# Turning attention probabilities on VectorE in 32 by 32 blocks, two heads at a time, instead of on TensorE through a PSUM bank

## The reference

```
proj = rms_norm_2(x, norm_g) @ w_in             # 2048 -> 11264 columns: q k v z_a u_b v_b z_b g_a g_b
q, k = rms_norm_2 per head of 128               # 8 heads
att = moba_attention(q, k, v)                   # 256 tokens are one block of 256: plain causal attention
y_a = (att * silu(z_a)) @ w_proj_a
sgu = spatial_gating(gelu(u_b), gelu(v_b), ...)
y_b = (sgu * silu(z_b)) @ w_proj_b
x + (sigmoid(g_a) * y_a + sigmoid(g_b) * y_b) @ w_out
```

## Time and profile before

| | |
|---|---|
| median of three runs | 2683.2 us |
| span of the profiled execution, first to last instruction | 2681.3 us |
| TensorE busy | 2675.3 us (100%) |
| VectorE busy | 1907.4 us (71%) |
| ScalarE busy | 1293.7 us (48%) |
| DMA | 192 GB/s mean, 56.6% of 16 engines on the weight queue |
| granted TensorE clock over the span | 1.000 |

### The profile page before, as it was taken

One profiled execution on the slowest core, in us unless ns is written; L12 is line 12 of the kernel. 1 busy time (PEld: TensorE's weight loads), 2 busy tenths in 40 slices (PEclk: granted clock), 3 DMA queues, 4 the chain that ended last, 5 costly groups with the idle time before them and its releaser, 6 DMA issues.

```text
span 2681.3 us, 31135 instructions
## 1 busy us (share of the span) xinstructions
PE 2675.3 (100%) x11969; PEld 2215.8 (83%) x11969; DVE 1907.4 (71%) x2594; ACT 1293.7 (48%) x1635; POOL 289.4 (11%) x263
## 2 busy tenths in 40 slices
PE   9999999999999999999999999999999999999999
PEld 7888888888888888888888888888888888888887
DVE  6887867666766777776777676667668867765564
ACT  7765544444444454444544444444445546544442
POOL 4741100000000010000100000000011001000000
PEclk9999999999999999999999999999999999999999
DMA  8555665555655556555556555556555655555554
GB/s 258 186 173 185 209 203 188 189 188 190 205 187 191 202 184 208 195 197 195 182 191 205 200 189 188 189 189 204 188 188 180 210 182 175 174 201 191 188 188 157
DMA packets 268148, 515.58 MB, mean 192 GB/s; under 512 B 8498, under 2 KB 28260, under 8 KB 267492
## 3 DMA queue, kind: packets, MB, share of 16 engines
q1 hardware_dynamic: 267732, 513.34, 56.6%
q10 hardware_dynamic: 272, 0.26, 0.0%
HBM read 511.47 MB, written 2.10 MB: 192 GB/s over the span
## 4 chain that ended last, share of the span: by engine, by line
PE 99%; DMA 0%; DVE 0%; SPq 0%; DVEq 0%; issue 0%
PE bank L819 33%; PE bank L821 32%; PE bank L820 32%; PE bank L870 0%; PE bank L888 0%; PE bank L1050 0%; DMA x_res<-in_x 0%; DMA w_raw<-in_ab_w_in 0%; PE bank L1011 0%; PE bank L1064 0%; PE bank L1037 0%; PE bank L1071 0%; PE bank L1079 0%; PE bank L1080 0%; PE bank L1038 0%; PE bank L1078 0%
## 5 line engine op out<-in xcount | busy, mean ns | idle before, releaser
L798 DVE TENSOR_TENSOR w_lo<-w_raw,w_hi 128x1024 fp32r<-128x1024 f32 x950 | 1182.1, 1264 | 471.8 <-ACT w_hi L780 465.8
L780 ACT ACTIVATE w_hi<-w_raw 128x1024 fp32r<-128x1024 f32 x954 | 973.3, 1056 | 594.5 <-PE bank L821 419.6
L819 PE MATMUL bank<-w_hi,A_lo 128*128 128x512 f32 x2432 | 952.2, 392 | 0.7 <-DVE w_lo L788 0.7
L821 PE MATMUL bank<-w_hi,A_hi 128*128 128x512 f32 x2432 | 947.1, 389 | 0.0
L820 PE MATMUL bank<-w_lo,A_hi 128*128 128x512 f32 x2432 | 946.6, 389 | 0.0
L819 PE MATMUL bank<-w_hi,B_lo 128*128 128x512 f32 x1408 | 548.7, 390 | 0.0
L821 PE MATMUL bank<-w_hi,B_hi 128*128 128x512 f32 x1408 | 547.9, 389 | 0.0
L820 PE MATMUL bank<-w_lo,B_hi 128*128 128x512 f32 x1408 | 547.8, 389 | 0.0
L819 PEld LDWEIGHTS bank<-w_hi,A_lo 128*128 128x128 f32 x2432 | 456.7, 188 | 96.4 <-DVE w_lo L788 2.1
L821 PEld LDWEIGHTS bank<-w_hi,A_hi 128*128 128x128 f32 x2432 | 456.5, 188 | 95.5
L820 PEld LDWEIGHTS bank<-w_lo,A_hi 128*128 128x128 f32 x2432 | 456.8, 188 | 93.2
(11 more groups left out here) (180 smaller groups left out, 1005.5 us busy)
## 6 DMA issues: line engine op xcount, KB each, us to landing
w_raw<-in_ffn_w SPq DMA_DIRECT2D x256, 1024.0 KB, 5.1
w_raw<-in_w_in SPq DMA_DIRECT2D x88, 1024.0 KB, 5.0
w_raw<-in_sc_w_in SPq DMA_DIRECT2D x48, 1024.0 KB, 5.1
w_raw<-in_ab_w_out SPq DMA_DIRECT2D x16, 1024.0 KB, 5.0
w_raw<-in_sc_w_out SPq DMA_DIRECT2D x16, 1024.0 KB, 5.0
w_raw<-in_w_out SPq DMA_DIRECT2D x16, 1024.0 KB, 5.1
w_raw<-in_ab_w_in SPq DMA_DIRECT2D x26, 512.0 KB, 5.0
w_raw<-in_ab_w_in SPq DMA_DIRECT2D x8, 1024.0 KB, 5.1
```

What stands on the lines that cost most here:

```text
L780: e.activation(w_hi[:, s % SPLIT_SLOTS, :], raw_step(s), ACT.Copy).then_inc(hi_made, 1)
L798: e.tensor_tensor(w_lo[:, slot, :], raw_step(s), w_hi[:, slot, :].bitcast(F32), ALU.subtract).then_inc(lo_made, 1)
L819: e.matmul(ps, lo[:, kt, tok], wh, start=first, stop=False)
L821: ins = e.matmul(ps, hi[:, kt, tok], wh, start=False, stop=last)
```

## The change

The probabilities of two heads, which lie side by side in `scores_flat` as six blocks of 128 by 128, are turned by VectorE. One instruction takes 32 partitions and a column strip of 32 from each of the six blocks (32 by 192 elements) and writes them transposed to `both_probs`. A pair needs 16 instructions, spread over five steps (3, 3, 3, 3 and 4). TensorE's 24 transposes, the eight uses of an auxiliary bank for their results and ScalarE's eight copies go. `probs_made` is now said by VectorE, once for a pair, behind the last of the 16.

The placement by `ATT_RATE` (0.76 tasks a step) is replaced by a fixed plan of ten steps a pair. Pair p begins at step f = 10p: scores at f and f+1, exp at f+2 and f+3, turn at f+4 to f+8, values at f+9 and f+10. Step f+10 is also the first of the next pair. The last values stand in step 40.

Scores of a head no longer wait for TensorE's turn of head h-2, but for `probs_made` of the pair before, on VectorE itself. The first turn of a pair waits for the exp of its second head and for the last values of the pair before, because `both_probs` has one copy.

```
@@ -126,16 +126,21 @@
...
-ATT_TASKS = []
-for _h in range(HEADS + 1):
-    ATT_TASKS += [("scores", _h)] * (_h < HEADS) + [("turn", _h - 1)] * (_h > 0)
-    ATT_TASKS += [("exp", _h)] * (_h < HEADS) + [("values", _h - 1)] * (_h > 0)
-ATT_RATE = 0.76
+PAIR_STEPS = 10
+PAIR_TURNS = 5
+ATT_AT = {}
+for _pair in range(HEADS // 2):
+    _first = PAIR_STEPS * _pair
+    for _n in range(2):
+        ATT_AT.setdefault(_first + _n, []).append(("scores", 2 * _pair + _n))
+        ATT_AT.setdefault(_first + 2 + _n, []).append(("exp", 2 * _pair + _n))
+        ATT_AT.setdefault(_first + 4 + PAIR_TURNS + _n, []).append(("values", 2 * _pair + _n))
+    for _n in range(PAIR_TURNS):
+        ATT_AT.setdefault(_first + 4 + _n, []).append(("turn", (_pair, _n)))
 
 
 def att_tasks(r, i):
-    step = 8 * (r - 8) + i
-    return ATT_TASKS[int(ATT_RATE * step):int(ATT_RATE * (step + 1))] if 8 <= r < 14 else []
+    return ATT_AT.get(8 * (r - 8) + i, [])
...
...
@@ -317,7 +320,7 @@
         small = sbuf("small", 512)
         neg_half = sbuf("neg_half", 16)
         z = sbuf("z", Z_SLOTS * NT * CH).rearrange("p (s t c) -> p s t c", s=Z_SLOTS, t=NT)
-        prod_rows = sbuf("tap_product", 2 * TOK)
+        prod_rows = sbuf("tap_product", 2 * 3 * P)
         scores_flat = sbuf("scores", 2 * 3 * P)
         halves = {}
         for name in ("A", "B"):
...
@@ -338,7 +341,7 @@
         band0 = gain_row[:, 0:4 * TOK].rearrange("p (g t) -> p g t", g=4)
         band1 = gain_row[:, 4 * TOK:4 * TOK + 4 * P].rearrange("p (g t) -> p g t", g=4)
         pool_w = acc_flat[:, 0:D].rearrange("p (g c e) -> p g c e", g=4, c=2)
-        tap_slots = [prod_rows, scores_flat[:, 0:2 * TOK]]
+        tap_slots = [prod_rows[:, 0:2 * TOK], scores_flat[:, 0:2 * TOK]]
         SPAD = SHORT_K - 1
         short_in = conv_in_flat[:, 0:GK * (TOK + SPAD)].rearrange("p (b t) -> p b t", b=GK)
         short_out = conv_out_flat[:, 0:GK * TOK].rearrange("p (b t) -> p b t", b=GK)
...
@@ -355,7 +358,8 @@
         x_T = conv_out_flat[:, GK * TOK:(GK + 2) * TOK].rearrange("p (k t) -> p k t", k=2)
         ws_T = ws_flat.rearrange("p (g c) -> p g c", g=HEADS)
         scores = scores_flat.rearrange("p (s c) -> p s c", s=2)
-        probs_T = prod_rows
+        both_scores = scores_flat.rearrange("p (b t) -> p b t", b=6)
+        both_probs = prod_rows.rearrange("p (b t) -> p b t", b=6)
         merged = acc
 
         small_at, small_cols = {}, {}
...
@@ -438,7 +442,7 @@
                               [("gelu", 8), ("gelu", 9), ("gelu", 10)] + [(11, tt) for tt in tiles] +
                               [("gelu", 12)] + [(13, tt) for tt in tiles])
         exp_made = signal("exp_made", [(h,) for h in range(HEADS)])
-        probs_made = signal("probs_made", [(h,) for h in range(HEADS)])
+        probs_made = signal("probs_made", [(pair,) for pair in range(HEADS // 2)])
 
         dve_took = signal("dve_took", [(c, tt) for c in range(N_CHUNKS) if evicted_by(c) == "DVE" for tt in tiles])
         lo_cast = signal("lo_cast", CAST)
...
@@ -1064,20 +1068,14 @@
                 e.matmul(ps[:, 0:TOK], q_T[:, h, P:TOK], k_T[:, h, :], start=True, stop=True)
                 e.matmul(ps[:, TOK:3 * P], q_T[:, h, 0:P], k_T[:, h, 0:P], start=True,
                          stop=True).then_inc(aux_filled("sc", h), 1)
-            elif task == "turn":
-                b4 = aux_begin("pt", h)
-                e.wait_ge(exp_made.sem, exp_made.of(h))
-                for b in range(3):
-                    ins = e.transpose(b4[:, b * P:(b + 1) * P], scores[:, h % 2, b * P:(b + 1) * P], ident)
-                ins.then_inc(aux_filled("pt", h), 1)
             elif task == "values":
                 b4 = aux_begin("av", h)
-                e.wait_ge(probs_made.sem, probs_made.of(h))
+                e.wait_ge(probs_made.sem, probs_made.of(h // 2))
                 e.wait_ge(act_took.sem, act_took.of(C_L2 + 5, 1))
-                c = slice(h * HD, (h + 1) * HD)
-                e.matmul(b4[:, 0:HD], probs_T[:, 2 * P:3 * P], v_tok[:, 0, c], start=True, stop=True)
-                e.matmul(b4[:, HD:2 * HD], probs_T[:, 0:P], v_tok[:, 0, c], start=True, stop=False)
-                e.matmul(b4[:, HD:2 * HD], probs_T[:, P:2 * P], v_tok[:, 1, c], start=False,
+                c, b = slice(h * HD, (h + 1) * HD), 3 * (h % 2)
+                e.matmul(b4[:, 0:HD], both_probs[:, b + 2, :], v_tok[:, 0, c], start=True, stop=True)
+                e.matmul(b4[:, HD:2 * HD], both_probs[:, b, :], v_tok[:, 0, c], start=True, stop=False)
+                e.matmul(b4[:, HD:2 * HD], both_probs[:, b + 1, :], v_tok[:, 1, c], start=False,
                          stop=True).then_inc(aux_filled("av", h), 1)
 
 
...
@@ -1344,11 +1342,6 @@
                             ins = e.activation(part, part, ACT.Exp, bias=cols(2, "bias", h)[:, n:n + 1], scale=SCALE,
                                                accum_out=cols(2, "total", h)[:, n:n + 1])
                         ins.then_inc(exp_made(h), 1)
-                    elif task == "turn":
-                        e.wait_ge(aux_filled.sem, aux_filled.of("pt", h))
-                        if h > 0:
-                            e.wait_ge(aux_filled.sem, aux_filled.of("av", h - 1))
-                        e.activation(probs_T[:, 0:3 * P], aux_bank("pt", h)[:, 0:3 * P], ACT.Copy).then_inc(probs_made(h), 1)
                 if (r, i) in AO_AT:
                     j = AO_AT.index((r, i))
                     e.wait_ge(ao_turned.sem, ao_turned.of(j))
...
@@ -2062,7 +2055,22 @@
                                                  ALU.add, ALU.mult)
                 ins.then_inc(sgu_made(j, tt), 1)
 
+        def turn_probs(e, pair, n):
+
+            if n == 0:
+                e.wait_ge(exp_made.sem, exp_made.of(2 * pair + 1))
+                if pair > 0:
+                    e.wait_ge(aux_filled.sem, aux_filled.of("av", 2 * pair - 1))
+            for m in range(16 * n // PAIR_TURNS, 16 * (n + 1) // PAIR_TURNS):
+                here, there = (slice(32 * q, 32 * q + 32) for q in divmod(m, 4))
+                ins = e.transpose(both_probs[there, :, here], both_scores[here, :, there])
+            if n == PAIR_TURNS - 1:
+                ins.then_inc(probs_made(pair), 1)
+
         def dve_attention(e, task, h):
+            if task == "turn":
+                turn_probs(e, *h)
+                return
             s = scores[:, h % 2, :]
             parts = (s[:, TOK:3 * P], s[:, 0:TOK])
             if task == "scores":
...
@@ -2070,7 +2078,7 @@
                 e.wait_ge(set_up.sem, set_up.of("mask2"))
                 e.wait_ge(aux_filled.sem, aux_filled.of("sc", h))
                 if h >= 2:
-                    e.wait_ge(aux_filled.sem, aux_filled.of("pt", h - 2))
+                    e.wait_ge(probs_made.sem, probs_made.of(h // 2 - 1))
                 e.tensor_tensor(s, aux_bank("sc", h)[:, 0:3 * P], mask, ALU.add).then_inc(masked(h), 1)
                 e.wait_ge(masked.sem, masked.of(h))
                 e.reduce_max(top[:, 0:1], parts[0], axis=AXIS.X)
```

More of the change, by code:

```diff
@@ L513, in aux_done @@
                 return conv_fed.sem, conv_fed.of(*key)
-            said = {"win": pooled_made, "ln": ln_made, "silu": aff_made, "bg": y_made, "sgu": sgu_made, "sc": masked, "pt": probs_made}
+            said = {"win": pooled_made, "ln": ln_made, "silu": aff_made, "bg": y_made, "sgu": sgu_made, "sc": masked}
             if kind in said:
```

32 lines of the change are left out of this document (10 added, 22 removed).

## The result

The changed kernel takes 2697.44 us (median of 5 runs, 2695.3 to 2697.6) against 2683.2 (now 5 runs too, 2682.73 to 2683.88): ratio 1.0050, 95% interval 1.0039 to 1.0060. It is 14.2 us slower. The forecast was 2692.0 with a range of 2686 to 2698, so time and direction are inside it, but the likeliest case, 2689 to 2695, gave only 8.8 us and was missed. The missing five are a rival's. The profiled execution has a span of 2695.8 us, 14.5 more than before. Outside the attention stretch nothing moved: up to 2178 us TensorE is busy for 2175.66 us, before 2175.34, and from the turn of `z` behind step 49 (L874, before L870) to the end it is 348.0 us in both.

The account below looks back on a forecast made before the run. TensorE's own stream of matmuls was taken as the bound; -3.0 removed plus waits of 2.9, 5.4 and 3.3 gave +8.6 us, 2691.8 at the median, with some tenths for exposed weight loads 2692, range 2686 to 2698.

Parts of the forecast that it names:

- the likeliest case: Whole kernel: the forecast's own case of waits at values, 2692 us, own range 2689 to 2695, chance 0.55.
- Place and mechanism: Values of heads 0, 2 and 4: TensorE waits for VectorE's transposes queued behind a chunk-end gelu tied to TensorE's eviction.
- The removal, -3.0 us: TensorE's turns of eight heads go: 0.37 us a head, 3.0 us in all.
- rival 3: Low parts come late too and loads slide; following chunks lose 2 to 3 us more each, 2698 to 2703; chance 0.06.
- The cost of a transpose, 0.37: VectorE's 32 by 192 transpose: 0.37 us each, between 303 and 436 ns; 23.7 us for all 64.
- Pair 0: Steps 0 to 10: transposes end 11.06 us after step 7 starts, TensorE wants them at 8.16; wait 2.9 us.
- Pair 1: Steps 10 to 20: transposes end 19.0 us after step 15 starts, TensorE wants them at 13.6; wait 5.4 us.
- Pair 2: Steps 20 to 30: transposes end 23.3 us after step 23 starts, TensorE wants them at 20.0; wait 3.3 us.
- Pair 3: Steps 30 to 40: transposes end 9.9 us after step 36 starts, TensorE needs them at 10.9; no wait, 1 us spare.
- Rival 1: TensorE's clock falls in a wait: 1.9 us at steps 10 to 20, 5.7 at all three; 2694 to 2697; chance 0.25.
- Signs: New profile: pauses of 2 to 6 us before values of heads 0, 2, 4; transpose 0.35 to 0.39; TensorE busy 3 less.
- Rivals 2 and 3: First: VectorE early enough, TensorE never waits, 2680.2 us, chance 0.12. Second: late low parts, 2698 to 2703, chance 0.06.

Follow-up runs that it names:

- values later: Changed kernel with the values tasks one, two or three steps later: 2686.55, 2681.88 and 2681.94 us.
- turn in three steps: Changed kernel with a pair's 16 transposes in three steps (5, 5 and 6 at f+4 to f+6) instead of five, values steps unchanged: 2681.53 us.
- the load alone: Kernel before, keeping its turn on TensorE, plus 64 VectorE transposes of a constant into unused columns, which nobody waits for: 2684.24 us.
- The pauses filled with work: Changed kernel plus 24, 46 and 24 identity transposes on TensorE ahead of the wait for heads 0, 2 and 4: 2692.62 us.
- transposes ahead of gelu: Changed kernel with VectorE's three transposes in steps 7 and 15 before gelu's first operation instead of behind gelu: 2693.45 us.

## Why the prediction was right where it was, and where it fell short

**Place and mechanism: right.** Pauses before the values of heads 0, 2 and 4, the longest at head 2, none at the others, each ended by a signal that is queued behind the gelu and what VectorE does after it. Moving the demand (values later) and moving the signal (turn in three steps) both take the pauses away, and the load alone (transposes in the kernel before) brings none of them: shown from three sides.

**The removal, -3.0 us: the size is that of the rows, the yield isn't.** Once the waits at values are gone (values two or three steps later, turn in three steps), only 1.1 to 1.8 us of the 3.0 arrive. The prediction's forecast let TensorE's saving arrive in full, and late low parts stood only in rival 3. The traces hold the rest. Start to start, the late beginnings at L823, each with the 0.1 us that the next matmul is late behind it, come to 1.8 us with values two steps later, 2.0 with three and 1.5 with the turn in three steps, against 0.2 before. With the 3.0 removed that makes the stretch shorter by 1.4, 1.2 and 1.7 us; measured are 1.4, 1.2 and 1.8.

**The cost of a transpose, 0.37: right** (370 ns; bounds were 303 and 436).

**The waits, 2.9 + 5.4 + 3.3 = 11.6: measured 3.3 + 6.1 + 3.2 = 12.6.** Each is taken from start to start less one cadence (2206.49 to 2210.03 less 0.23, and so on). Pair 0: the last transpose was forecast for P(7)+11.06 and came at +11.4, P(7) being 2198.55 (the first operation of gelu, 2204.01, less the 5.46 of the earlier trace rows). The small terms were too small: gelu's multiplication followed by transposes took 1.26 from start to start (2204.74 to 2206.00), a low part followed by transposes likewise 1.26 (2207.14 to 2208.40), not the 1.14 between two operations of a kind. Pair 1: forecast +19.0, measured +19.6; the same terms make gelu's multiplication end 0.4 us later, and ScalarE's high part 21 and VectorE's low part behind it start as much later. The exp left its place in step 18, as said. Pair 2: the wait is right (3.2 for 3.3) with some luck, as both of its ends were too early. The gating was put at 1.0 us of TensorE by a misreading of the earlier trace rows: the profile counts each of these float32 matmuls twice, so 32 are two gatings and not four, and one takes 1.8 us (2268.89 to 2270.59, and 0.1 on the matmul behind).

```profile
2268.89 1.95 PE L1015 MATMUL bank<-conv_in,ws_T 128*128 128x128 f32 x16
2270.59 0.48 PE L823 MATMUL bank<-w_hi,A_lo 128*128 128x512 f32 x1
```

TensorE was therefore at the values at P(23)+20.9 and not +20.0, P(23) being 2260.73 by gelu's first operation at 2266.19. VectorE's last transpose came at +23.9 and not +23.3, by the same 1.26 in place of 1.14.

Pair 3: no wait, and half a microsecond of the one that was to spare, seen on VectorE and then on TensorE:

```profile
2315.33 1.53 DVE L2066 STREAM_TRANSPOSE tap_product<-scores 32x192 f32<-32x192 f32 x4
```

```profile
2317.33 0.38 PE L1076 MATMUL bank<-gain_row,tap_product 128*128 128x128 f32 x2
```

**The step that failed: that the clock holds.** Rival 1, with 0.25, had this: "5.7 if it happens at all three". It happened at all three, for 5.1 us. I had held 1.00 because the rows have no pause in mid-kernel, which was no evidence for it. The failed step is thus a term put at nothing: the forecast has no cost for the clock. Its 8.6 us plus 1.0 of waits plus 5.1 of clock is 14.7; the spans differ by 14.5. The pauses filled with work give the same sum without the clock, 12.6 - 3.0 = 9.6, and measured 9.6. The rival's own time, 2694 to 2697, lies just below the 2697.44 measured. It took some back because VectorE and ScalarE would catch up; nothing of that is seen in the sum, probably as VectorE's next signal comes a pair later and is again tied to an eviction of TensorE.

The Trainium skill, "TensorE: Matmul & The Clock Gate", section "Why this matters for your kernels", warned that idle gaps between bursts return the engine to the lower rate; behind all three pauses of the changed kernel it did (a granted clock of 0.66, 0.55 and 0.68 in the five microseconds behind them). It deserved more than a quarter.

**Signs.** TensorE's busy time was to go down by 3 us and went up by 2.7. The sign was badly chosen: busy time counts matmuls at whatever clock, and 5.1 us of slow ones hide the 3.0 removed. In the turn in three steps it reads 2673.7, 1.6 below; up to 2178 us, where the kernels are the same, it is 0.9 above, so differences of a microsecond in busy time say little here.

**Rivals 2 and 3.** Never a wait: wrong for the edit as made, though the mean load did allow it, as the turn in three steps shows. Late low parts: none in the changed kernel, as was argued against that rival: its pauses give VectorE the time; they appear once the pauses are gone.

## What to carry to other kernels

When work moves to an engine with room, ask where its signal stands in that engine's queue and which operation in front of it waits for the other engine; the share of busy time says nothing of that. Price a pause of TensorE as the pause plus a possible stretch at 1.2 GHz behind it, here 1.6 to 1.9 us each, and look for a place for the producer before the hole in its queue, or for the consumer a step or two later. Cheap idle work in the pause keeps the clock, but the pause itself is the larger part.

## What the runs showed of the hardware

- When the clock fell depended on the pause. It read 1.00 during the one of 3.15 us, and about the first microsecond behind it ran at full cadence (to 2211.0). Behind the pauses of 5.95 us and, with values one step later, 3.83 us, already the first matmuls were slow (0.77 us for a group of two instead of 0.46). Behind 1.89 us (transposes ahead of gelu) it stayed at 1.00.
- One and the same pause of 3.01 us was followed by 1.2 GHz in one profile and by 2.4 in another. The changed kernel's five times fall into 2695.3 and 2695.6 against 2697.4 to 2697.6, a distance of the size of one slow stretch, and the two lower ones have a granted clock of 0.998 over the span against 0.997. That it is one such stretch is likely and not shown, as they have no trace.
- Identity transposes held the clock: 24, 46 and 24 of them in the pauses, and the window 2178 to 2334 ran at 1.00; the pause filled with 46 is the one behind which every unfilled trace shows the lower level. The Trainium skill, "TensorE: Matmul & The Clock Gate", section "Part 4: PE-mode transpose", says that transposes don't count as busy for the gate in the same way. The trace of this kernel disagrees. They took 0.11 to 0.12 us each (24 in 2.78 us).
- A VectorE transpose of 32x192 behind an ordinary operation starts about 0.12 us later than another ordinary one there does (1.26 us start to start against 1.14), and among themselves they follow at 0.38.
